# Norm roots, weight halves, side by side products and freed blocks in a two-block transformer kernel

## The reference

```
def _rmsnorm(x, g):
    xf = x.astype(jnp.float32)
    y = xf * lax.rsqrt(jnp.mean(xf * xf, axis=-1, keepdims=True) + EPS)
    return (y * g.astype(jnp.float32)).astype(x.dtype)
...
        hn = _rmsnorm(h, attn_norm[layer])
        ...
        h = h + mix
        h = h + _swiglu(_rmsnorm(h, ffn_norm[layer]), f_w_gate_up[layer], f_w_down[layer])
    return _rmsnorm(h, final_norm)
```

## Time and profile before

| | us |
|---|---|
| median of three runs | 3132.38 |
| lowest, highest | 3124.88, 3133.9 |
| the profiled execution | 3136.3 |
| its span | 3134.5 |
| PE busy, mean granted clock | 2918.3, 0.94 |
| DVE busy | 1978.9 |
| ACT busy | 1466.4 |

### The profile page before, as it was taken

One profiled execution on the slowest core, in us unless ns is written; L12 is line 12 of the kernel. 1 busy time (PEld: TensorE's weight loads), 2 busy tenths in 40 slices (PEclk: granted clock), 3 DMA queues, 4 the chain that ended last, 5 costly groups with the idle time before them and its releaser, 6 DMA issues.

```text
span 3134.5 us, 57237 instructions
## 1 busy us (share of the span) xinstructions
PE 2918.3 (93%) x19610; PEld 2711.0 (86%) x19610; DVE 1978.9 (63%) x4205; ACT 1466.4 (47%) x2397; POOL 338.8 (11%) x167
## 2 busy tenths in 40 slices
PE   7889799999999998968999999999997899999998
PEld 6889699999988887858998999988886779987998
DVE  6545942886577676685597887466775655445554
ACT  5444344444455555444444444455554444443443
POOL 0003685000000000000277000000000000000000
PEclk9998899999999999889899999999998879995999
DMA  4434366445666663322456445676664315450444
GB/s 155 153 148 148 134 211 199 172 171 188 230 250 239 241 242 132 121 78 98 149 178 210 174 170 186 217 254 238 245 236 149 120 54 177 176 220 6 162 182 155
DMA packets 140448, 546.16 MB, mean 174 GB/s; under 512 B 15784, under 2 KB 81592, under 8 KB 83616
## 3 DMA queue, kind: packets, MB, share of 16 engines
q1 hardware_dynamic: 63216, 455.38, 40.1%
q10 hardware_dynamic: 73728, 67.14, 6.9%
q0 software_dynamic: 3376, 21.88, 1.8%
HBM read 505.53 MB, written 40.91 MB: 174 GB/s over the span
## 4 chain that ended last, share of the span: by engine, by line
PE 74%; DVE 9%; DMA 6%; ACT 5%; POOL 4%; issue 2%; SPq 0%; ACTq 0%; DVEq 0%
PE bank L699 22%; PE bank L700 21%; PE bank L701 21%; POOL wL L493 4%; PE bank L855 4%; ACT wH L483 3%; DVE wL L493 3%; DMA ring<-in_w_stream 3%; DMA act_parked<-act_out 2%; PE bank L756 2%; PE bank L774 2%; PE bank L765 1%; PE bank L712 1%; DVE act_out L1486 1%; DVE h L1518 1%
## 5 line engine op out<-in xcount | busy, mean ns | idle before, releaser
L493 DVE TENSOR_TENSOR wL<-ring,wH 128x1024 fp32r<-128x1024 f32 x744 | 906.9, 1225 | 750.9 <-ACT wH L483 750.3
L699 PE MATMUL bank<-hnH,wH 128*128 128x256 f32 x3648 | 1066.9, 292 | 61.2 <-DVE hnL L1492 44.1
L700 PE MATMUL bank<-hnL,wH 128*128 128x256 f32 x3648 | 1045.4, 287 | 0.0
L701 PE MATMUL bank<-hnH,wL 128*128 128x256 f32 x3648 | 1044.7, 286 | 0.0
L483 ACT ACTIVATE wH<-ring 128x1024 fp32r<-128x1024 f32 x864 | 906.3, 1055 | 274.0 <-DMA ring<-in_w_stream 128.6
L699 PEld LDWEIGHTS bank<-hnH,wH 128*128 128x128 f32 x3648 | 711.6, 195 | 71.8 <-issue 57.7
L700 PEld LDWEIGHTS bank<-hnL,wH 128*128 128x128 f32 x3648 | 714.5, 196 | 0.1
L701 PEld LDWEIGHTS bank<-hnH,wL 128*128 128x128 f32 x3648 | 712.8, 195 | 0.0
L699 PE MATMUL bank<-wH,wgtH 128*128 128x512 f32 x1024 | 400.1, 391 | 4.5 <-issue 4.5
L700 PE MATMUL bank<-wL,wgtH 128*128 128x512 f32 x1024 | 399.5, 390 | 0.0
L701 PE MATMUL bank<-wH,wgtL 128*128 128x512 f32 x1024 | 399.5, 390 | 0.0
(11 more groups left out here) (338 smaller groups left out, 3612.7 us busy)
## 6 DMA issues: line engine op xcount, KB each, us to landing
ring<-in_w_stream SPq DMA_DIRECT2D x432, 1024.0 KB, 4.9
act_parked<-act_out ACTq DMA_DIRECT2D x256, 128.0 KB, 3.6
act_in<-act_parked ACTq DMA_DIRECT2D x256, 128.0 KB, 2.7
sw_bias<-in_c_swa POOLq DMA_DIRECT2D x1, 4096.0 KB, 13.9
relb_rows<-rel_table POOLq DMA_DIRECT2D x1, 2048.0 KB, 9.6
h_parked<-h POOLq DMA_DIRECT2D x2, 1024.0 KB, 6.5
h_back<-h_parked POOLq DMA_DIRECT2D x2, 1024.0 KB, 6.3
od_relb<-relb_rows POOLq DMA_DIRECT2D x2, 1024.0 KB, 8.2
```

The source lines that it names most:

```text
L493: eng.tensor_tensor(wL[:, b % NBUF, :], raw(b), wH[:, b % NBUF, :].bitcast(F32), ALU.subtract).then_inc(w_low, 1)
L699: pe.matmul(dst, lh, rh, start=start, stop=False, skip_group_check=True)
L700: pe.matmul(dst, lh, rl, start=False, stop=False, skip_group_check=True)
L701: return pe.matmul(dst, ll, rh, start=False, stop=stop, skip_group_check=True)
```

## The change

The change has five parts.

- The root of a norm no longer takes the pending splits ahead of itself (except for mem and x0). They stand behind the second `hnH` on ACT and ahead of the fourth scaling on DVE. A 128 x 1 Sqrt at the start of the squares makes ACT load the table there, in all 13 norms.
- In ten norms (all but mix0, mem and x0) DVE adds squares 1 to 6 into square 0 as they come, six additions (`gather`), and PE sums two parts: that one and square 7. mix2's squares wait for each scaled chunk alone.
- The first three products behind a norm (LEAD) run chunk by chunk side by side in three banks.
- In the down projection the first two blocks of an output are free once PE has read them, not when the output is done.
- At the end of an expert layer three weight blocks are split ahead of the wait for the last value product.

```diff
 NORM_NO = {n[0]: i for i, n in enumerate(NORMS)}
+GATHERED = [n[0] for n in NORMS if n[0] not in ("mix0", "mem", "x0")]
+GATHERS = DC - 2
...
+LEAD = 3
...
                 blocks.append(((f"ffn{l}gu", m, b), (f"ffn{l}gu", m, b)))
-        lin(f"ffn{l}d", 8, "dve", per=3)
+        for m in range(8):
+            g((f"ffn{l}d", m), "dve")
+            for b in range(3):
+                blocks.append(((f"ffn{l}d", m, b), ("ffd", l, m, b) if b < 2 else (f"ffn{l}d", m)))
...
+            if key[0] == "ffd":
+                return NO[(f"ffn{key[1]}d", key[2])] - 0.5
...
+                elif key[0] == "ffd":
+                    eng.wait_ge(ffd_done, 16 * key[1] + 2 * key[2] + key[3] + 1)
...
                 i = NORM_NO[name]
+                if name in GATHERED:
+                    ps = bank(("norm", name))
+                    pe.wait_ge(gathered, GATHERS * (GATHERED.index(name) + 1))
+                    pe.matmul(ps[:, 0:T], ones, sq[:, 0, :], start=True, stop=False)
+                    pe.wait_ge(sq_done, DC * i + DC)
+                    pe.matmul(ps[:, 0:T], ones, sq[:, DC - 1, :], start=False, stop=True).then_inc(group_done, 1)
+                    return
                 norm(("norm", name), [sq[:, c, :] for c in range(DC)], sq_done, DC * i)
...
-                for m in ms:
+                ms = list(ms)
+                lead = ms[0:LEAD] if first is not None else []
+                held = [bank((name, m)) for m in lead]
+                for k in range(nk if lead else 0):
+                    for m, ps in zip(lead, held):
+                        blk = w((name, m, 0))
+                        if m == lead[0]:
+                            first(k)
+                        last = product(ps[0:width, 0:T], both(blk, FULL, slice(k * width, (k + 1) * width)),
+                                       both(src, FULL, k), k == 0, k == nk - 1)
+                        if k == nk - 1:
+                            last.then_inc(group_done, 1)
+                for m in ms[len(lead):]:
                     ps = bank((name, m))
...
                         blk = w((name, m, k // 8))
-                        if first is not None and m == ms[0]:
-                            first(k)
                         last = product(ps[0:width, 0:T], both(blk, FULL, slice(k % 8 * width, (k % 8 + 1) * width)),
                                        both(src, FULL, k), k == 0, k == nk - 1)
+                        if nk > DC and k in (7, 15):
+                            last.then_inc(ffd_done, 1)
                     last.then_inc(group_done, 1)
...
-                for m in range(FC):
-                    for s in range(2):
-                        ps = bank((f + "gu", m, s))
+                pairs = [(m, s) for m in range(FC) for s in range(2)]
+                held = [bank((f + "gu", m, s)) for m, s in pairs[0:LEAD]]
+                for k in range(DC):
+                    for (m, s), ps in zip(pairs, held):
...
-                        for k in range(DC):
...
             n96 = [3, 4]
-            for m in range(13):
-                lin("mla_in", [m], hn, width=96 if m in n96 else P,
-                    first=(lambda k: normed("mix2", k)) if m == 0 else None)
+            lin("mla_in", range(3), hn, first=lambda k: normed("mix2", k))
+            for m in range(3, 13):
+                lin("mla_in", [m], hn, width=96 if m in n96 else P)
                 if m == 6:
...
-                ps = take(key)
+                if key[0] == "norm" and key[1] not in ("mem", "x0"):
+                    assert rank[NO[key]] == reads[0] + 1, key
+                    reads[0] += 1
+                    act.wait_ge(group_done, NO[key] + 1)
+                    ps = psum[bank_of[NO[key]]]
+                else:
+                    ps = take(key)
                 act.activation(dst, ps[:, 0:T], ACT.Sqrt, bias=eps,
...
                 src = mem_raw if name == "mem" else h
+                act.activation(small[:, 81:82], eps, ACT.Sqrt)
                 for c in range(DC):
...
                         added(act, adds or order[order.index(name) - 1], c)
-                    if i and c == 0:
+                    if i and c == 0 and name != "mix2":
                         act.wait_ge(hn_done, DC * i)
...
                         high((memH if name == "mem" else hnH)[:, c, :], sq[:, c, :])
+                        if c == 1:
+                            feed(act, NO[("norm", name)] + 1)
...
                         split_high(act, b0 + N_KEYS + 3 + c)
-                fed[id(act)][0] = b0 + 2 * N_KEYS
+                for b in range(b0 + 2 * N_KEYS, b0 + 2 * N_KEYS + 3):
+                    split_high(act, b)
+                fed[id(act)][0] = b0 + 2 * N_KEYS + 3
                 act.wait_ge(v_done, (l + 1) * N_KEYS)
...
                 whole = name in ("final", "final2")
-                root(("norm", name))
+                n = NO[("norm", name)]
+                if name in ("mem", "x0"):
+                    feed(dve, n)
+                dve.wait_ge(read_by["act"], rank[n])
+                link(dve.reciprocal(root_sb, root_sb))
                 for c in range(DC + 1):
+                    if c == 3:
+                        feed(dve, n + 1)
                     if c < DC:
...
                                                  ALU.mult, ALU.mult).then_inc(hn_done if whole else values, 1)
+                        if name == "final":
+                            gather("mix2", c - 1)
                     if c and not whole:
...
-            def add(name):
+            def gather(name, c):
+
+                if name in GATHERED and 0 < c < DC - 1:
+                    done = GATHERS * GATHERED.index(name) + c - 1
+                    dve.wait_ge(sq_done, DC * NORM_NO[name] + c + 1)
+                    dve.wait_ge(gathered, done)
+                    dve.tensor_tensor(sq[:, 0, :], sq[:, 0, :], sq[:, c, :], ALU.add).then_inc(gathered, 1)
+
+            def add(name, nxt):
...
                     dve.tensor_tensor(h[:, m, :], h[:, m, :], ps[:, 0:T], ALU.add).then_inc(read_by["dve"], 1)
+                    gather(nxt, m - 1)
...
-                fed[id(dve)][0] = b0 + 2 * N_KEYS
+                for b in range(b0 + 2 * N_KEYS, b0 + 2 * N_KEYS + 3):
+                    split_low(dve, b)
+                fed[id(dve)][0] = b0 + 2 * N_KEYS + 3
...
                     dve.tensor_tensor(h[:, c, :], h_back[:, c, :], ps[:, 0:T], ALU.add).then_inc(read_by["dve"], 1)
+                    gather("final" if l else "mix1", c - 1)
...
-            add("mix2")
+            add("mix2", "ffn0")
```

More of the change, by code:

```diff
@@ L435, in build_stacks @@
         values, highs = sem("values"), sem("highs")
-        sq_done, hn_done = sem("sq_done"), sem("hn_done")
+        sq_done, hn_done, gathered = sem("sq_done"), sem("hn_done"), sem("squares_gathered")
         chain_v, chain_a = sem("chain_v"), sem("chain_a")
@@ L457, in build_stacks @@
         eps_set, sink_set = sem("eps_set"), sem("sink_set")
-        out_done = sem("out_done")
+        out_done, ffd_done = sem("out_done"), sem("ffn_down_block_done")
         def freed_by(b):
@@ L1700, in cross @@
                 attention(x)
-                add(x)
+                add(x, f"peer{l}")
             def ffn(l):
@@ L1715, in ffn @@
                 low(ff_aL[:, FC - 1, :], ff_f[:, (FC - 1) % 2, :], ff_aH[:, FC - 1, :]).then_inc(ff_low, 1)
-                add(f)
+                add(f, "final2" if l else "mix3")
             dve.wait_ge(con_in, 32)
@@ L1766, in _ @@
                                          ALU.subtract).then_inc(read_by["dve"], 1)
-            add("mix0")
+            add("mix0", "x0")
             cross(0)
@@ L1909, in _ @@
                 low_of(("yc", j), od_yL[:, j, :], od_yH[:, j, :])
-            add("mix1")
+            add("mix1", "x1")
             cross(1)
@@ L1946, in _ @@
             attention("swa")
-            add("mix3")
+            add("mix3", "ffn1")
             ffn(1)
```

18 lines of the change are left out of this document (13 added, 5 removed).

## The result

| | before | after |
|---|---|---|
| median of the first runs, us | 3133.14 (4) | 3085.41 (4) |
| lowest, highest | 3124.88, 3139.85 | 3071.83, 3110.29 |
| median with the later runs | 3134.3 (56) | 3086.2 (10) |
| the profiled execution, its span | 3136.3, 3134.5 | 3071.8, 3070.0 |
| mean granted clock of it | 0.94 | 0.953 |

The ratio is 0.9856, 95% interval 0.9812 to 0.9901. The forecast was 3110.3 with a range down to 3098: the direction was right, but the gain of some 48 us is twice the 22 that were forecast. The changed kernel's ten times fall into two heaps, six at 3072 to 3087 us and four at 3104 to 3118; the fast heap has the higher mean granted clock. The profiled execution was the fastest of all, so its trace shows more gain than the median.

A forecast was written before the change was run, and what follows sets the result against it. The prediction took PE as the bound, busy 2918.3 of 3134.5 us, with only its idle or half-clock time winnable. Its terms summed to 22.1 us, from the median 3132.38 to 3110.3 us, range 3098 to 3122.

The forecast's parts named there:

- roots earlier, five norms: Norms of peer0, x1, peer1, ffn0, ffn1: root 0.95 us earlier each, 4.8 us in all.
- mix3, final2: Norms after the down projection: roots no longer behind pending splits, 2.6 and 1.7 us gained.
- experts' end, mix1: Three blocks split before the last value product's wait, ring slot free some 6 us sooner: 5.2 us gained.
- final and mix2: Final's adds 1.9 us sooner without four splits in a row, mix2's overlapped squares 2.3 less: 4.2 us together.
- down projections: Blocks freed early close PE's wait for weight halves, 8.47 to 7.92 us per output: 7.7 us over two layers.
- side by side, behind eight norms: Three products per chunk fill PE's idle time at an unchanged 5.4 us of half clock: 0.4 us in all.
- all up to peer0's first product, without its root: Early losses: mix0 1.3, mem's table load 1.5, x0 0.2, x0's query 1.5 us.
- Rival (a): Convoy: blocks freed together make PE wait for the ring at nine starts, 40 us lost, 3150 us; chance 0.05.
- rival b: Half clock begins sooner or lasts 0.9 us longer at ten norms, taking 9 us: 3119 us; chance 0.17.
- Rival (d): Full clock holds through the norms, side by side worth 2 us at eight sites: 3096 us; chance 0.08.
- Rival (c): Down projection bound by the ring, so its 7.7 us are not gained: 3118 us; chance 0.15.
- (e): Gathers and semaphore hops lie on the path, roots come no sooner: 3120 us; chance 0.08 including mishaps.

The follow-up runs named there:

- mla_filled: Changed kernel plus one 128x128 fp32 product of constants per step of the MLA attention; median 3089.3 us against 3116.5 for the kernel before with the same filler.
- after_again: The changed kernel run once more, unedited: six runs from 3079.5 to 3118.2 us, the traced execution 3106.6 us with the MLA attention at half clock.
- two filled kernels: The kernel before and the changed kernel, each with one 128x128 product of constants per step of the MLA attention; medians 3116.5 and 3089.3 us.
- late_root: Changed kernel with every root again behind the pending splits and the table load behind the squares; median 3108.8 us.
- norm_filled: Changed kernel plus 128x256 products of constants where PE waits in the norms, before the gathered sum and before the first product; median 3092.1 us.
- no_gather: Changed kernel without the gathers, PE summing all eight squares itself; median 3109.0 us.

## Why the forecast was half of it

The step that failed is one without a term: the forecast held every stage that the change does not touch at its time, and so at its clock. The MLA attention won 20.8 us in the first trace and some 20 in the median, by a granted clock of 0.95 in place of 0.53 and with the same instructions. The terms that were summed came out at 22 to 24 us in the traces, forecast and as the three traces of the changed kernel (two, and mla_filled) have them against before:

| step | forecast | shown |
|---|---|---|
| roots earlier, five norms | 4.8 | 4.8 to 5.3 |
| mix3, final2 | 2.6, 1.7 | 3.0, 2.0 |
| experts' end, mix1 | 5.2 | 5.6 to 6.1 |
| final and mix2 | 4.2 | 4.8 |
| down projections | 7.7 | 7.4 |
| side by side, behind eight norms | 0.4 | 4 to 6 |
| side by side, behind mix1's inner norm | 0 | -2.7 to -3.6 |
| all up to peer0's first product, without its root | -4.5 | -6.3 to -7.1 |
| sum | 22 | 22 to 24 |
| clock of the experts' scores | 0 | 17.6, 5.3, 0.4 in the three traces |
| clock of the MLA attention | 0 | 20.8 in the first trace, some 20 in the median |

In after_again the two sums, 24 and 5.3, make up the 29.7 us between the profiled executions. The two filled kernels differ by 27; there the kernel before also lost 2.9 us in x0's query, at half clock for 6.8 us.

**Right, with its size.** The mechanism of the roots (reciprocal 3.63 us behind the last add, then 2.54 to 2.99), the experts' end with the ring transfer, and the spacing of the down projection's adds to 0.01 us. For mix3 and final2 the size is right, but late_root shows that the freed blocks bring most of it also without the moved root. Rival (a), the convoy, fell at its price of 40 us: behind none of the gathered norms did PE of the changed kernel wait over 0.8 us for a weight half. In small it came, in mix1, for some 3 us.

**Side by side, mis-sized.** This term reads that the half clock lasts the 5.4 us that it did "whatever PE runs in them". It does not: behind mix3's norm it was 3.2 us with 15 records, behind ffn0's 5.8 with 27. At the eight sites of three traces it ends 2.9 to 6.2 us behind the first product, after 13 to 29 records; the means are 4.8, 4.3 and 4.3 us, against 5.3 before. So PE's clock came back earlier on average, the start was worth 0.5 to 0.8 a site and not 0.05, and without it the earlier splits would have cost 1.3 a site. Rival (d) gave the direction; norm_filled shows its full price, some 1.5 us per site beyond the changed kernel.

**The early part, underestimated.** Mem's table load cost 1.5 to 1.7 us as forecast (PE waited 6.19 to 6.39 us for its first square, 4.73, and 4.68 in late_root). mix0 cost nothing clear where 1.3 was forecast: PE was ready for mem's sums at 48.3 to 49.4, before at 48.7 and 48.9. x0's query cost more than said, some 3 us from its first product to the attention, with 3.4 to 6.8 us at half clock. PE's first product there:

```profile
177.90 0.35 PE L709 MATMUL bank<-hnH,wH 128*128 128x256 f32 x1 [3.09 <-DVE wL L503]
```

**The clock of stages that the change does not touch, left out.** The forecast took the clock as something of the norms (rival b). But the trace of before had the MLA attention's loop at a mean clock of 0.53, and the page's two slices of that mixer at 8 and 7 tenths: some 20 us lay there, as the two kernels with fillers show. That the changed kernel sometimes keeps this clock was no part of the forecast's reasoning, and what in the change allows it stays open. Rival (b), a longer half clock in the norms, had the sign wrong. Rival (c) fell by the 7.92 spacing. Of (e), the gathers on the path, no_gather shows 0.7 us in mix1 and 1.5 in mix2; from mix1's first add to its root it took 7.2 us, where the forecast had 7.7 and 7.13 stood.

## What to carry to other kernels

Before a change is costed, list the stretches where the granted clock is under full and ask of each what would turn it: here a loop over three engines took 1.5 to 1.8 times as long at half clock, and a change that does not touch it let it keep the full clock in some executions. When a kernel's times form two heaps, compare the mean granted clock of each run, and hold the stage's clock by filler work in both kernels before the change is judged. An earlier root, with a split moved behind it, pays only if something covers the split in its new place: behind the norms three products side by side did. But blocks that are used side by side also come free at one instant, and what stands behind them in ACT's order waits for the ring.

## What the runs showed of the hardware

- Work that is thrown away can save time: 32 fp32 products of 128 columns in the steps of one attention made the kernel before 18 us faster. Twelve products of 256 columns in a norm's waits (22 in mix2) held PE's clock at 2.4 GHz through the norm (granted clock 1.00 where it had been 0.50 for 2.9 to 6.2 us).
- The window attention stood at 1.2 GHz for some 65 us or more in all 17 traces, with and without fillers, while PE's records show it busy throughout.
- In the experts' score products one or two stretches of 10.2 us at half clock come and go between traces, at about 5 us each.
- The same program differed by up to 46 us between executions (3071.8 and 3118.2), and the mean granted clock (0.953 and 0.938) went with it.
